# Two attentions of a single-core kernel: probabilities normalised ahead of their transposes, and values matmuls that give the result already turned

## What is computed

```python
s = jnp.einsum('bhqd,bhkd->bhqk', qb, k) * scale
s = s + cq[..., :, None] - cf[..., None, :]
s = jnp.where(kpos[None, :] <= qpos[:, None], s, NEG_INF)
p = jax.nn.softmax(s, axis=-1)
out = jnp.einsum('bhqk,bhkd->bhqd', p, v)
...
return jnp.concatenate([pool_out, attn_out], axis=-1) @ w_out
```

```python
logits = einsum('bthe,btkhe->bhtk', qb, kg) * scale + bias
logits = jnp.where(valid[:, None], logits, -jnp.inf)
p = jax.nn.softmax(logits, axis=-1)
o = jnp.einsum('bhtk,btkhe->bthe', p, vg)
...
return out @ w_out
```

## Time and profile before

| | |
|---|---|
| three runs | 1361.49, 1361.87, 1361.95 us, median 1361.87 |
| the profiled execution | 1361.84 us, span of its instructions 1359.9 us |
| TensorE busy | 1351.5 us, 99% of the span |
| VectorE, ScalarE, GpSimd busy | 939.2, 674.7, 49.7 us |
| DMA | 257.81 MB read, 192 GB/s over the span |
| granted TensorE clock, mean | 0.999 of 2.4 GHz |

### The profile page before, as it was taken

The page is one execution under the profiler, slowest core; times in us unless marked ns, Lnnn a source line. Parts: engine busy times, 40 slices in busy tenths (PEclk is TensorE's granted clock), DMA queues, the critical chain, the costliest instruction groups (busy, mean ns, idle before and its releaser), DMA issues. The chain is left out here.

```text
span 1359.9 us, 18452 instructions
## 1 busy us (share of the span) xinstructions
PE 1351.5 (99%) x7481; PEld 1173.6 (86%) x7481; DVE 939.2 (69%) x1106; ACT 674.7 (50%) x842; POOL 49.7 (4%) x77
## 2 busy tenths in 40 slices
PE   9999999999999999999999999999999999999998
PEld 8888888898888899888888888888888888888886
DVE  7777556776666778866666766666768877676665
ACT  6525434364444542654444554445554444554443
POOL 1010000020000100020000000000000000000000
PEclk9999999999999999999999999999999999999999
DMA  8638464545555473346454454455473555465540
GB/s 317 252 134 308 152 242 155 217 147 225 189 197 195 147 263 125 124 171 248 186 186 186 155 217 186 186 188 215 161 272 120 218 205 200 155 229 199 192 155 31
DMA packets 38483, 260.07 MB, mean 191 GB/s; under 512 B 4449, under 2 KB 4625, under 8 KB 8705
## 3 DMA queue, kind: packets, MB, share of 16 engines
q1 hardware_dynamic: 34848, 244.50, 48.4%
q0 software_dynamic: 3552, 14.40, 3.0%
HBM read 257.81 MB, written 2.64 MB: 192 GB/s over the span
## 5 line engine op out<-in xcount | busy, mean ns | idle before, releaser
L820 DVE TENSOR_TENSOR wlo<-raw,whi 128x2048 fp32r<-128x2048 f32 x228 | 519.9, 2288 | 72.7 <-ACT whi L539 72.5
L539 ACT ACTIVATE whi<-raw 128x2048 fp32r<-128x2048 f32 x228 | 433.8, 1909 | 34.6 <-DMA raw<-slabs_dram 26.7
L1386 PE MATMUL acc<-whi,ht 128*128 128x512 f32 x544 | 214.2, 394 | 0.0
L1387 PE MATMUL acc<-wlo,ht 128*128 128x512 f32 x544 | 212.4, 390 | 0.0
L1388 PE MATMUL acc<-whi,ht 128*128 128x512 f32 x544 | 211.9, 389 | 0.0
L1615 PE MATMUL mm<-xt,whi 128*128 128x512 f32 x848 | 201.5, 390 | 0.0
L1615 PE MATMUL tp<-xt,whi 128*128 128x512 f32 x848 | 201.4, 390 | 0.0
L1615 PEld LDWEIGHTS tp<-xt,whi 128*128 128x128 f32 x848 | 158.5, 188 | 33.2 <-DVE hid L935 0.6
L1615 PEld LDWEIGHTS mm<-xt,whi 128*128 128x128 f32 x848 | 158.7, 188 | 33.0 <-DVE hid L935 0.3
L935 DVE TENSOR_TENSOR hid<-mm,hid 128x512 f32<-128x512 f32 x58 | 40.1, 691 | 190.9 <-ACT hid L602 190.9
L602 ACT ACTIVATE hid<-mm 128x512 f32<-128x512 f32 x58 | 34.6, 597 | 265.3 <-PE mm L1622 255.6
(11 more groups left out here) (249 smaller groups left out, 1602.5 us busy)
## 6 DMA issues: line engine op xcount, KB each, us to landing
raw<-slabs_dram SPq DMA_DIRECT2D x228, 1024.0 KB, 4.9
vec<-vectors_dram POOLq DMA_DIRECT2D x12, 512.0 KB, 5.4
raw<-first_dram SPq DMA_DIRECT2D x8, 384.0 KB, 5.6
tables_dram<-table_dram POOLq DMA_DIRECT2D x1, 1536.0 KB, 9.3
hlf<-slabs_dram SPq DMA_DIRECT2D x1, 1024.0 KB, 7.8
vec<-forget_dram POOLq DMA_DIRECT2D x1, 1024.0 KB, 9.3
h<-x_dram POOLq DMA_DIRECT2D x2, 512.0 KB, 6.1
htf<-tables_dram POOLq DMA_DIRECT2D x1, 1024.0 KB, 8.8
```

The costliest lines, as they stand in the source:

```text
L539: nc.scalar.activation(whi[:, m % RING, :], raw[:, m % RAW, :], ACT.Copy).then_inc(hi_done, 1)
L820: nc.vector.tensor_tensor(wlo[:, m % RING, :], raw[:, m % RAW, :], whi[:, m % RING, :], ALU.subtract).then_inc(lo_done, 1)
L1386: nc.tensor.matmul(out, a[0], b[0], start=first, stop=False)
L1387: nc.tensor.matmul(out, a[0], b[1], start=False, stop=False)
```

## The change

- VectorE no longer scales the result of the values matmuls. `normalized(g)` takes the reciprocals of the row sums and multiplies the probabilities in `hid` by them in place, 128x512 elements for groups 0 and 1, 128x1024 for groups 2 and 3, and signals `norm_ready`. `turn_probs(g)` waits for that instead of `p_ready`.
- `values(g)` swaps its sides: the values of a head are stationary, the turned probabilities move (128 columns each). The result is channels by queries. In att1, where a head has 64 channels, even heads write partitions 0 to 63 and odd heads 64 to 127 of the same bank.
- `turn_att`, its transposes and the buffer `att` are gone. `to_xt(g)` on ScalarE and VectorE writes `xt` straight from `mm`, once for each group: 128x256 elements in att1, 128x512 in att2.
- The orders of the three queues are written anew around this, and the slab splits are put elsewhere. `v_tile1` is no longer cut by transposes and waits for `xt_ready` 1.

The core of the diff (left out: the semaphore names, ScalarE's `to_xt`, argument lists):

```diff
+                def normalized(g):
+
+                    dve.wait_ge(a.p_ready, g + 1)
+                    r, keys = RS + 4 * g, P * (GROUPS[g][0] + 1)
                     step(nc.vector.reciprocal(st[:, REC:REC + 4], st[:, r:r + 4]))
-                    if g == 2:
-
-                        dve.wait_ge(a.xtp_ready, tiles // 4)
-                    hh = GROUPS[g][1]
-                    nc.vector.tensor_tensor(by_head(att[:, hh * 4 * width:(hh + 1) * 4 * width]),
-                                            by_head(mm[:, g % 2, 0:4 * width]),
-                                            spread(st[:, REC:REC + 4], [[1, 4], [0, width]]), ALU.mult)\
-                      .then_inc(a.att_ready, 1)
-                    dve.wait_ge(a.att_ready, g + 1)
-
-                def turned(t):
-                    for j in range(tiles // 4):
-                        tp_to_xt(a.hi_ready, tiles // 4 * t + j, base + 4 * j, t, a.xt_ready)
+                    p = by_head(hid[:, place_of(g):place_of(g) + 4 * keys])
+                    nc.vector.tensor_tensor(p, p, spread(st[:, REC:REC + 4], [[1, 4], [0, keys]]), ALU.mult)\
+                      .then_inc(a.norm_ready, 1)
+                    dve.wait_ge(a.norm_ready, g + 1)
...
                 if a is att1:
                     maxima(0)
                     maxima(1)
                     evacuate(w_in, len(IN_UNITS) - 2, IN_UNITS[-2])
+                    normalized(0)
+                    normalized(1)
                     splits.upto(end + 2)
                     maxima(2)
                     between()
+                    normalized(2)
                     maxima(3)
-                    scaled(0)
-                    scaled(1)
+                    to_xt(0)
+                    normalized(3)
+                    to_xt(1)
                     splits.upto(end + 4)
-                    turned(0)
-                    scaled(2)
+                    to_xt(2)
                     splits.upto(end + RING - 1)
-                    scaled(3)
+                    filler()
+                    to_xt(3)
                     splits.upto(end + RING)
-                    filler()
-                    turned(1)
                     return
...
                 maxima(0)
                 maxima(1)
+                normalized(0)
+                normalized(1)
+                between()
                 splits.upto(end + 1)
-                between()
-                scaled(0)
-                scaled(1)
+                to_xt(0)
+                to_xt(1)
                 maxima(2)
-                turned(0)
                 maxima(3)
+                normalized(2)
                 filler()
+                splits.upto(end + 2)
+                normalized(3)
+                splits.upto(end + 3)
+                to_xt(2)
                 splits.upto(end + 4)
-                scaled(2)
-                scaled(3)
-                turned(1)
+                to_xt(3)
                 splits.upto(end + RING)
...
                 def turn_probs(g):
                     t, hh = GROUPS[g]
-                    pe.wait_ge(a.p_ready, g + 1)
+                    pe.wait_ge(a.norm_ready, g + 1)
...
-                        pe.wait_ge(a.att_ready, g - 1)
-                    for i in range(4):
-                        for kb in range(t + 1):
-                            p = place_of(g) + kb * N + i * P
-                            ins = nc.tensor.matmul(mm[:, g % 2, i * width:(i + 1) * width], ptf[:, p:p + P],
-                                                   value(kb, 4 * hh + i), start=kb == 0, stop=kb == t)
+                        pe.wait_ge(a.xt_ready, g - 1)
+                    for pair in range(2):
+                        for i in (2 * pair, 2 * pair + 1):
+                            for kb in range(t + 1):
+                                p = place_of(g) + kb * N + i * P
+                                if a is att1:
+                                    out = mm[i % 2 * DH1:(i % 2 + 1) * DH1, g % 2, pair * P:(pair + 1) * P]
+                                else:
+                                    out = mm[:, g % 2, i * P:(i + 1) * P]
+                                ins = nc.tensor.matmul(out, value(kb, 4 * hh + i), ptf[:, p:p + P],
+                                                       start=kb == 0, stop=kb == t)
...
                     values(0)
                     values(1)
                     out_slab(out, 0, 1)
-                    turn_att(0)
                     values(2)
                     turn_probs(3)
+                    pe.wait_ge(a.xt_ready, 1)
                     out_slab(out, 0, 2)
                     values(3)
+                    pe.wait_ge(a.xt_ready, 2)
                     out_slab(out, 0, 3)
                     out_slab(out, 1, 0)
-                    turn_att(1)
                     out_slab(out, 1, 1)
-                    pe.wait_ge(a.xt_ready, 2)
+                    pe.wait_ge(a.xt_ready, 4)
...
                 values(0)
                 values(1)
                 scores(3)
-                filler(lambda: turn_att(0))
-
+                filler()
                 turn_probs(2)
 
-                pe.wait_ge(a.xt_ready, tiles // 4)
+                pe.wait_ge(a.xt_ready, 1)
                 out_slab(out, 0, 0)
+                out_slab(out, 0, 1)
                 values(2)
                 turn_probs(3)
-                out_slab(out, 0, 1)
+                pe.wait_ge(a.xt_ready, 2)
+                out_slab(out, 0, 2)
                 values(3)
-                out_slab(out, 0, 2)
-                turn_att(1)
                 out_slab(out, 0, 3)
 
-                pe.wait_ge(a.xt_ready, tiles // 4 + 1)
+                pe.wait_ge(a.xt_ready, 3)
                 out_part(out, 1, 0, 0)
                 out_part(out, 1, 1, 0)
-                pe.wait_ge(a.xt_ready, tiles // 2)
+                pe.wait_ge(a.xt_ready, 4)
...
-            def v_tile1(turn):
-
-                pe.wait_ge(att2.att_ready, 1)
+            def v_tile1():
+
+                pe.wait_ge(att2.xt_ready, 1)
                 pe.wait_ge(a_in.evac, LAST_A - 1)
                 u = A_UNITS[LAST_A]
-                token_part(LAST_A % 2, u.m, u.i, range(4), release=True)
-                turn()
-                token_part(LAST_A % 2, u.m, u.i, range(4, KD), release=True)
+                token_part(LAST_A % 2, u.m, u.i, range(KD), release=True)
```

More of the change, by code:

```diff
@@ L654, in gelu_gate, with attention @@
                 ins.then_inc(mixb.gate_ready, 1)
-            def attention(a, tiles, base, end, between=None):
+            def attention(a, end, between=None):
                 def exps(g):
@@ L749, in pooled @@
                                          scale=st[:, PSC + g:PSC + g + 1]).then_inc(pool.hi_ready, 1)
-            attention(att1, WIDTH // P, WIDTH // P, w_in.end, pooled)
+            attention(att1, w_in.end, pooled)
             norm(n0, squares=False)
@@ L772, in _ @@
                     relus(INDEX_AFTER[n])
-            attention(att2, D // P, 0, a_in.end)
+            attention(att2, a_in.end)
             norm(n3)
@@ L1044, in normalize_v, with attention @@
                   .then_inc(vln.done, 1)
-            def attention(a, width, tiles, base, end, post, between, filler):
+            def attention(a, end, post, between, filler):
                 def maxima(g):
@@ L1244, in first_sums @@
                 layer_stats(l0, 0)
-            attention(att1, DH1, WIDTH // P, WIDTH // P, w_in.end, forget_and_mask, pooled, first_sums)
+            attention(att1, w_in.end, forget_and_mask, pooled, first_sums)
             layer_rest(l0, n0, 0, 0)
@@ L1317, in bias_and_select @@
                 step(nc.vector.tensor_tensor(s, s, spread(sel, [[0, 4], [1, keys]]), ALU.add))
[L1319 removed]
+            attention(att2, a_in.end, bias_and_select,
                       lambda: evacuate(a_in, LAST_A - 1, A_UNITS[LAST_A - 1]),
@@ L1799, in fused, with attention @@
                     tail_by_tile()
-            def attention(a, score, value, width, out, between, filler, following, v_ready):
-                tiles = HEADS * width // P
+            def attention(a, score, value, out, between, filler, following, v_ready):
                 def scores(g):
@@ L1824, in turn_probs @@
                             pe.wait_ge(a.pt_ready, n - 1)
-                        if g == (3 if a is att1 else 2) and kb < tiles // 4:
-                            pe.wait_ge(a.xt_ready, kb + 1)
                         for i in range(4):
```

68 lines of the change are left out of this document (31 added, 37 removed).

## The result

The change makes the kernel slower: median 1369.55 us of six runs (1366.04 to 1370.28) against 1361.80 us (1361.49 to 1362.17), a ratio of 1.005 with a 95% interval of 1.004 to 1.006. The forecast was 1366.1 us with a range from 1363.5 to 1370.0. The single runs of the changed kernel lie 4.2 us apart, those of the kernel before 0.7 here and up to 1.3 in later sets. The mean granted clock of the six runs goes with their times: 0.999 in the run of 1366.04 us, 0.998 at 1367.08, 0.997 at 1369.05, and 0.995 in the three from 1370.04 to 1370.28.

The account below looks back on a forecast made before the run. The prediction took TensorE to bound the kernel: waits less removed work gave +1.0 us in the first attention and +3.3 in the second, so 1361.84 + 4.3 = 1366.1 us, with a range from 1363.5 to 1370.0.

Parts of the forecast that it names:

- What bounds the kernel: TensorE, busy 1351.5 of 1359.9 us; its removed work is gained, its new waits paid in full, other engines' work counts nothing.
- The hole in the first attention: TensorE's transposes of group 2 wait for VectorE's normalisation, which comes after the pool's low parts: +3.4 us.
- The hole in the second: Second attention: TensorE's transposes of group 2 wait for a normalisation behind the maxima of groups 2 and 3: +3.5 us.
- The three small waits: Second attention: TensorE waits 0.5 us for group 1's normalisation, 0.6 for the fourth slab's split, 0.4 for the first sum.
- (a): The transposes of the result taken off TensorE: 0.9 us saved in the first attention, 1.7 in the second.
- (b): First attention's 48 values matmuls run as pairs in column halves: 5.4 us become 2.7, saving 1.5 us after the visits.
- the rival that halves run in turn: First attention's values matmuls in column halves run one behind the other, saving nothing: 1368.8 us; chance 25%.
- the visits: Going into column halves and out again in the first attention's values matmuls: three times 0.4 us, 1.2 us.
- The sum, 1366.1 us: +1.0 us in the first attention and +3.3 in the second, +4.3 on the profiled execution's 1361.84.
- the granted clock falls in a hole: Rival: work behind a hole runs at up to twice its time, about 1368.5 us for one, 1371 for both; chance 10%.
- My own case: The forecast without its rivals, from 1364.4 us (visits free, holes 0.5 shorter) to 1367; chance 50%.
- the rival that it would be faster: VectorE reaches both normalisations of group 2 in time, holes together under 2.6 us: 1357.7 or 1359.2 us; chance 7%.

Follow-up runs that it names:

- best2: best with one late split ahead of VectorE's and ScalarE's last xt write, one inside norm 3, and maxima of group 2 earlier in the second attention: 1359.12 us.
- busy: The changed kernel with 14 throw-away identity matmuls ahead of the transposes of group 2 in both attentions: 1365.59 us.
- early2: The changed kernel; in the second attention VectorE splits the second output slab and normalises group 2 ahead of the maxima of group 3: 1365.77 us.
- best: The changed kernel with the orders of TensorE, ScalarE and VectorE fitted to the new chain in both attentions: 1366.38 us.
- busy4: The changed kernel with 4 throw-away matmuls, where busy has 14, ahead of the transposes of group 2 in both attentions: 1367.06 us.
- early1: The changed kernel; in the first attention VectorE normalises group 2 ahead of the pool's low parts: 1365.52 us.
- both: The changed kernel with the edits of early1 and early2 together: 1362.61 us.

## Why the prediction was right, and where it was not

- **What bounds the kernel**: right. Every kernel above moves by what its TensorE work and waits sum to; VectorE has 3.5 us more to do (942.7 against 939.2), and best2 shows that this costs nothing by itself.
- **The hole in the first attention, +3.4**: right. Worked out from 62.73 to 66.1, measured at 66.12, behind a normalisation that starts at 64.84. **The hole in the second, +3.5**: right in length (3.4 by starts) and in its cause. The three small waits were right too: 0.6 for group 1 where 0.5 stood, 0.65 for the split ahead of slab (0,3) where 0.6 stood, 0.3 for the first turned sum where 0.4 stood.
- **(a) and (b), the work taken out**: in (b) the pairs are right, and the rival that halves run in turn, 25%, is refuted (1.96 against 1.09 us). The rule cited there from the Trainium skill ("TensorE: Matmul & The Clock Gate", The mechanism) is about the order of matmuls and of weight loads; that column halves would gain little was my own conclusion from it, and the same page reports a gain for column tiles (Measured speedup vs the span model), with which the measurement agrees. In the product, 48 x 0.11 is 5.3 and not 5.4, which changes nothing. In the first attention (a) and (b) stood at 0.9 + 1.5 = 2.4; at full clock, with its hole of 3.3 us, the stretch of busy and early2 is 0.6 over before, so they saved 2.7: the visits were dear at 0.4 each, about 0.3 is my estimate from this. In the second, (a) stood at 1.7, and 1.8 came: busy has 3.4 + 0.6 + 0.65 + 0.3 = 4.95 us of waits by starts and a stretch 3.2 over before. The transposes themselves say the same. The 24 matmuls that project the values of tile 1 take 560.95 - 554.38 = 6.57 us with 8 transposes among them in the kernel before (the 560.95 is in the earlier trace rows) and 558.45 - 552.88 = 5.57 without them in best2, which makes 1.0 for 8 of them.
- **The sum, 1366.1 us**: it is, to 0.5 us, the time of the kernel at full clock. Six runs of the change begin at 1366.04, and busy, which holds the clock up, has 1365.59.
- **What the prediction had wrong** is the chance of the rival "the granted clock falls in a hole", 10%; the forecast itself put the clock at nothing, and of the 7.7 us between the medians it lacks 3.4. The rival's place, its price (1.7 to 3.6 us for one hole; measured 1.6 and 2.9) and its total (1368.5 or 1371; the median is 1369.55) were right or nearly so. I had the row for it, the tail of the kernel where the clock fell 3.3 us after the last matmul, called the holes "as close as can be", and then gave it a tenth. I also read the 3.3 us as if it were a fixed delay. The traces show falls 2.5 us (best), 2.6 and 4.4 (the change), 3.7 (busy4) and 4.5 us (early1) after TensorE fell idle, so that one row could not say whether a hole of 3.2 us is long enough.
- **The number** is right by the range, and that is luck. My own case ended at 1367. The range went up to 1370.0 for the halves in turn, which didn't happen, and for one fall of the clock, where the profiled execution has two; three of the six runs lie above it.
- **The rival that it would be faster** named its condition rightly, holes of under 2.6 us together; best2 is this case, and shows that the normalisation itself needn't cost anything.

What stays open: why the same hole of 3.2 us brings the clock down in some executions and not in others. And a run that only takes the transposes out or puts them in wasn't made; what they are worth is read from the timelines.

## What to carry to other kernels

Work that is moved off the bound engine pays only if the engine that takes it over does it in time: look for what stands ahead of the new operation in that engine's queue, and put the operation ahead of everything that nobody waits for yet, weight splits above all. When an order is fitted, read the list of waits again after every step, since the next thing that is late may stand well behind the place of the change, and it can cost more than all that was won. And price a hole on TensorE as long as those here (2.4 to 3.5 us) with what follows it at half clock, not with its length alone; throw-away matmuls in the hole show in one run how much of the loss is clock.

## What the runs showed of the hardware that I had not expected

- The clock behind a hole isn't settled by the hole's length. It fell at holes of 3.2 and 3.3 us (the change), 3.3 (early1), 3.5 (best) and 2.4 us (busy4, second attention); it stayed full behind 3.2 us (early2), 2.3 us (busy4, first attention) and 1.6 us (early2, both). Nor does it fall at a fixed time after TensorE falls idle: 2.5 to 4.5 us.
- Where the clock fell while TensorE was still idle, 0.7 us before it went on (the second hole of the change) or 1.1 us (best), it stayed at half for 6.7 to 6.8 us; where it fell only 1.2 to 1.3 us after TensorE had gone on (the first hole of the change, early1, busy4), for 3.4 us. These are five falls; what decides between the two wasn't tested.
- Halves of the array by columns run in nearly full pairs, with heads that alternate between them two or four records at a time: 16 records in 1.09 us against 1.96 us in one half.
